# The last two weight blocks of an output projection, multiplied chunk by chunk

## The reference, cut to what matters

```python
def rmsnorm(x, g):
    xf = x.astype(jnp.float32)
    y = xf * lax.rsqrt(jnp.mean(xf * xf, axis=-1, keepdims=True) + RMS_EPS)
    return (y * g.astype(jnp.float32)).astype(x.dtype)

f = swiglu(rmsnorm(h, ffn1_g_pre[l]), ffn1_w_gu[l], ffn1_w_down[l])
h = h + MACARON_W * rmsnorm(f, ffn1_g_post[l])
m = hybrid_mixer(rmsnorm(h, mix_g_pre[l]), mix_w_in[l], ...)
h = h + rmsnorm(m, mix_g_post[l])
```

## Time and profile before

| | |
|---|---|
| median of 3 runs | 1300.17 us (1297.37 to 1300.36) |
| the profiled execution, its time | 1300.92 us |
| its span | 1299.2 us |
| PE busy | 1236.9 us (95%) |
| POOL busy | 493.9 us (38%) |
| ACT busy | 448.5 us (35%) |
| DVE busy | 414.1 us (32%) |
| mean granted clock of TensorE | 0.973 |

### The profile page before, as it was taken

The page is one execution under the profiler, slowest core; times in us unless marked ns, Lnnn a source line. Parts: engine busy times, 40 slices in busy tenths (PEclk is TensorE's granted clock), DMA queues, the critical chain, the costliest instruction groups (busy, mean ns, idle before and its releaser), DMA issues.

```text
span 1299.2 us, 15515 instructions
## 1 busy us (share of the span) xinstructions
PE 1236.9 (95%) x5659; PEld 1001.6 (77%) x5659; DVE 414.1 (32%) x708; ACT 448.5 (35%) x688; POOL 493.9 (38%) x238
## 2 busy tenths in 40 slices
PE   7999999999998989999989899889899999999997
PEld 5788888888886667777767877667788888888886
DVE  4432222210017353544351424521722323230004
ACT  3433333331134344453333444423532323231113
POOL 4344444444442331222133673214244444444442
PEclk9999999999998988999889899999999999999999
DMA  5233333222231221111102342102133333322211
GB/s 183 65 98 97 97 97 97 97 97 97 97 97 49 65 70 45 49 49 49 66 28 89 114 151 81 58 32 86 61 98 98 97 97 97 97 96 91 93 60 65
DMA packets 83319, 108.76 MB, mean 84 GB/s; under 512 B 8686, under 2 KB 53836, under 8 KB 83276
## 3 DMA queue, kind: packets, MB, share of 16 engines
q1 hardware_dynamic: 83120, 108.14, 25.6%
q10 hardware_dynamic: 156, 0.04, 0.0%
HBM read 106.06 MB, written 2.10 MB: 83 GB/s over the span
## 4 chain that ended last, share of the span: by engine, by line
PE 42%; issue 38%; POOL 14%; DVE 4%; ACT 2%; POOLq 0%; DVEq 0%; ACTq 0%
PE bank L1409 13%; POOL w_lo L563 13%; PE bank L1411 13%; PE bank L1410 13%; PE bank L1427 1%; PE bank L1417 1%; DVE acc L983 1%; DVE acc L980 0%; PE bank L1434 0%; DVE h L1040 0%; DVE f_fin L1394 0%; DVE qm_lo L1176 0%; ACT xh L640 0%; DVE tmp L1168 0%; ACT w_hi L627 0%
## 5 line engine op out<-in xcount | busy, mean ns | idle before, releaser
L563 POOL TENSOR_TENSOR w_lo<-raw,w_hi 128x1024 fp32r<-128x1024 f32 x176 | 428.2, 2433 | 750.1 <-ACT w_hi L627 750.1
L1409 PE MATMUL bank<-xh,w_hi 128*128 128x512 f32 x992 | 394.3, 397 | 16.6 <-DVE xl L969 14.5
L1411 PE MATMUL bank<-xh,w_lo 128*128 128x512 f32 x992 | 389.7, 393 | 0.0
L1410 PE MATMUL bank<-xl,w_hi 128*128 128x512 f32 x992 | 389.2, 392 | 0.0
L627 ACT ACTIVATE w_hi<-raw 128x1024 fp32r<-128x1024 f32 x176 | 186.3, 1058 | 512.6 <-PE bank L1411 508.1
L1409 PEld LDWEIGHTS bank<-xh,w_hi 128*128 128x128 f32 x992 | 188.2, 190 | 63.2 <-issue 17.0
L1411 PEld LDWEIGHTS bank<-xh,w_lo 128*128 128x128 f32 x992 | 187.9, 189 | 39.9
L1410 PEld LDWEIGHTS bank<-xl,w_hi 128*128 128x128 f32 x992 | 188.3, 190 | 37.6
L1409 PE MATMUL bank<-mid_hi,w_hi 128*128 (+1 forms) x352 | 138.9, 394 | 0.0
L1411 PE MATMUL bank<-mid_hi,w_lo 128*128 (+1 forms) x352 | 138.0, 392 | 0.0
L1410 PE MATMUL bank<-mid_lo,w_hi 128*128 (+1 forms) x352 | 136.6, 388 | 0.0
(11 more groups left out here) (234 smaller groups left out, 1337.1 us busy)
## 6 DMA issues: line engine op xcount, KB each, us to landing
raw<-in_ffn_w_gu SPq DMA_DIRECT2D x176, 256.0 KB, 2.9
raw<-in_ffn_w_down SPq DMA_DIRECT2D x88, 256.0 KB, 2.8
raw<-in_mix_w_in SPq DMA_DIRECT2D x48, 256.0 KB, 2.8
raw<-in_mem_w_kv SPq DMA_DIRECT2D x32, 256.0 KB, 3.3
raw<-in_mix_w_out SPq DMA_DIRECT2D x16, 256.0 KB, 3.0
raw<-in_mem_w_q SPq DMA_DIRECT2D x16, 256.0 KB, 3.2
raw<-in_mem_w_o SPq DMA_DIRECT2D x16, 256.0 KB, 2.8
x_tok<-in_x SPq DMA_DIRECT2D x4, 512.0 KB, 5.0
```

The costliest lines, as they stand in the source:

```text
L563: gp.tensor_tensor(w_lo[:, n % SPLIT, :], raw[:, n % RAW, :], w_hi[:, n % SPLIT, :].bitcast(F32), ALU.subtract).then_inc(lo_ready, 1)
L1409: pe.matmul(dst, w[0], x[0], start=start, stop=False, skip_group_check=loose)
L1410: pe.matmul(dst, w[0], x[1], start=False, stop=False, skip_group_check=loose)
L1411: return pe.matmul(dst, w[1], x[0], start=False, stop=stop, skip_group_check=loose)
```

## The change

A new function of PE, `closing_out`, takes the last two weight blocks of each output projection together: for each bank first the three products of block n-1, then the three of block n. Each bank so ends with its six products. In bank 7, between the two triples, stand the four products that sum `acc`, with the flag that clears bank 0; the squares of banks 6 and 7 are summed after the last product, as before. In the SwiGLU the loop has one turn fewer, and three blocks are written out behind it. On ACT one rounding is no longer issued before the squares. The diff, without its unchanged parts:

```diff
...
                 round_to(OUT_END[s])
                 act.preload_act_table(ACT.Sqrt)
-                round_to(OUT_END[s] + 1)
                 act.wait_ge(hacc_ready, H_ADDS * (s + 1))
                 for m in range(DC):
                     wait_out(act, s, m)
...
                 for _ in range(products):
                     pe.matmul(dst[:, :], ones[:, :], ones[:, 0:1].to_broadcast([P, SEQ]), start=True, stop=True)
-            def token_sums(dst, parts):
+            def token_sums(dst, parts, first=True, last=True):
...
                     for semaphore, count in waits:
                         pe.wait_ge(semaphore, count)
                     for t in range(TC):
-                        last = pe.matmul(dst[:, t:t + 1], square[:, t * P:(t + 1) * P], ones[:, 0:1],
-                                         start=n == t == 0, stop=n == len(parts) - 1, skip_group_check=True)
-                return last
+                        done = pe.matmul(dst[:, t:t + 1], square[:, t * P:(t + 1) * P], ones[:, 0:1],
+                                         start=first and n == t == 0, stop=last and n == len(parts) - 1,
+                                         skip_group_check=True)
+                return done
             def spread(dst, src):
...
                     pe.wait_ge(saved_a, 1)
                     turn_h(2)
                 token_sums(out_bank(s, 0), [
-                    (fsq(DC - 2), [(f0_saved, s + 1), (fsq_ready, DC * s + DC - 1)]),
-                    (acc, [(facc_ready, F_ADDS * (s + 1))]),
-                    (fsq(DC - 1), [(fsq_ready, DC * (s + 1))])]).then_inc(fstat, 1)
+                    (fsq(DC - 2), [(fsq_ready, DC * s + DC - 1)]),
+                    (fsq(DC - 1), [(fsq_ready, DC * (s + 1))])], False).then_inc(fstat, 1)
                 if s == SUBLAYERS - 1:
                     pe.wait_ge(saved_a, 2)
                     turn_h(3)
...
                 if DC - 1 in ms:
                     last.then_inc(w_used, 1)
+            def closing_out(s, n, x):
+                w = [weights(n - 1), weights(n)]
+                for m in range(DC):
+                    cols = slice(m * P, (m + 1) * P)
+                    for j in range(2):
+                        last = three(out_bank(s, m)[:, :], (w[j][0][:, cols], w[j][1][:, cols]), x[j],
+                                     False, j == 1, True)
+                        if m == DC - 1:
+                            last.then_inc(w_used, 1)
+                            if j == 0:
+                                token_sums(out_bank(s, 0), [
+                                    (acc, [(f0_saved, s + 1), (facc_ready, F_ADDS * (s + 1))])], True, False)
+                    if m < DC - 1:
+                        last.then_inc(out_done, 1)
             def swiglu(s, up, down):
                 first = 2 * FG * (s // 3)
                 first_block(s, up, 0)
...
                 pe.wait_ge(up_scaled, first + 2 * FG - 1)
                 pe.wait_ge(midl_done, first + 1)
                 out_block(s, down, hidden(0), True, False, free={4: (up_scaled, first + 2 * FG + 1)})
-                with pe.Fori(0, (FC - 2) // 4) as i:
+                with pe.Fori(0, (FC - 6) // 4) as i:
                     for k in range(4):
                         pe.wait_ge(midl_done, at_turn(i, 4, first + 2 + k))
                         out_block(s, down + 1 + k, hidden(at_turn(i, 4, 1 + k)), False, False, i, 4)
+                for k in range(FC - 5, FC - 2):
+                    pe.wait_ge(midl_done, first + 1 + k)
+                    out_block(s, down + k, hidden(k), False, False)
                 pe.wait_ge(midl_done, first + FC)
-                out_block(s, down + FC - 1, hidden(FC - 1), False, True)
+                closing_out(s, down + FC - 1, (hidden(FC - 2), hidden(FC - 1)))
                 out_stat(s)
             def fill(turn):
...
                 for k in range(2):
                     free = {0: (gfactor, GLA_H), 2: (mem_l, DC)} if k == 0 else {}
                     group_block(B_OUT + 2 + k, k, 0, (fox_hi, fox_lo), free=free, last_chunk=DC)
-                for c in range(4, DC):
+                for c in range(4, DC - 2):
                     pe.wait_ge(y_l, Y_FOX + c - 3)
-                    out_block(1, B_OUT + c, (xh[:, c, :], xl[:, c, :]), False, c == DC - 1)
+                    out_block(1, B_OUT + c, (xh[:, c, :], xl[:, c, :]), False, False)
+                pe.wait_ge(y_l, Y_GLA)
+                closing_out(1, B_KV - 1, [(xh[:, c, :], xl[:, c, :]) for c in (DC - 2, DC - 1)])
                 out_stat(1)
             def memory():
...
                 attention(MEM_B)
                 free = {3: (pt_l, N_UNITS), 5: (y_l, Y_GLA + 7), 6: (y_l, Y_GLA + DC)}
-                for c in range(DC):
+                for c in range(DC - 2):
                     pe.wait_ge(y_l, Y_GLA + c + 1)
-                    out_block(2, B_MO + c, (xh[:, c, :], xl[:, c, :]), c == 0, c == DC - 1,
+                    out_block(2, B_MO + c, (xh[:, c, :], xl[:, c, :]), c == 0, False,
                               free={} if c else free, ms=range(DC) if c else range(3, DC))
+                pe.wait_ge(y_l, Y_GLA + DC)
+                closing_out(2, B_UP2 - 1, [(xh[:, c, :], xl[:, c, :]) for c in (DC - 2, DC - 1)])
                 out_stat(2)
```

## The result

The changed kernel takes 1317.47 us (median of 4 runs, 1314.87 to 1322.54), the kernel before, in runs beside it, 1298.77 us. The ratio is 1.0157 (95% interval 1.0130 to 1.0184): slower by 18.7 us, the difference of the medians. The prediction had 1322.0 us, 21.8 us over before, with a range from 1316 to 1328, and slower at 0.97.

A forecast was written before the change was run, and what follows sets the result against it. The prediction took TensorE (PE), busy for 95% of the span, as the bound. Added waits 15.3, clock 6.0 and ends 0.5 made 21.8 us, giving a median of 1322.0 us, with a range from 1316 to 1328.

The forecast's parts named there:

- The wait that is added: Before block n-1 of each projection, PE waits for block n's weights: 3.80 or 3.86 us each, 15.3 us together.
- The clock: Behind each of the four added pauses PE's clock falls: 1.5 us each, 6.0 us, one pause bounded by 0 and 2.0.
- The ends: After each projection's last product, POOL's residues delay the update of h: three ends of 0.17 us, 0.5 us together.
- E + 7.43: At the first projection's end, POOL's two residues end 7.43 us after E, the end of the last weight product before.
- The sum: Whole kernel: 15.3 + 6.0 + 0.5 = 21.8 us slower, median 1322.0 us; the forecast's chance was 0.70.
- Rival 2: The clock costs more, 2.0 us or more at each pause and some low stretches at ends: 1328 us, chance 0.09.
- Rival 1: At the four pauses the clock doesn't fall, or falls while PE stands: 1316 us, chance 0.13.
- Rivals 3 and 5: Respectively: PE waits for `acc` in the closing stretch, 1325 us, 0.04; the wait comes only before block n, 1319 us, 0.02.
- Rival 4: Faster: three ends without the wait for DVE, the sums and one rounding give 8.4 us, 1291.8 us; chance 0.02.

The follow-up runs named there:

- e1: The kernel before, with only PE's wait for the last block's weights added ahead of block n-1 at each projection; 1322.05 us, ratio 1.0191.
- e2: The changed kernel, with a third slot for each projection's last block so its rounding waits for block n-3, not n-2; 1299.68 us, ratio 1.0012.
- e3: The changed kernel, with the sums of `acc` put back behind the last product; 1319.64 us, ratio 1.0153.
- e10: The changed kernel, with DVE's eight operations on GLA's output waiting for POOL to complete the mixer's fourth output block; ratio 1.0154.
- e4: The kernel before, with ACT's part of the change alone: the next stage's first block is rounded behind the squares; 1295.02 us, ratio 0.9968.
- e7: The kernel before with ACT's part of the change alone, the same kernel as e4 measured once more; 1294.32 us, ratio 0.9965.
- e8: The kernel before, with ACT's first rounding behind the squares, its second behind the next pre-norm's second chunk, and DVE waiting for POOL in the mixer; ratio 0.9961.

## Why the prediction was right, and where it was off

- **The wait that is added** (15.3 us): the four steps from block n-2 to block n-1 grew by 15.4 us. Right, and e1 shows that it is the cause.
- **The clock** (6.0 us, 1.5 for each pause): too small. In the changed kernel the 48 products took 12.2 us more, of which the sums are 4.2 by e2, so the clock took 8.0; in e1 it took 6.3, in e3 9.6, in e10 8.3. The mean is 8.0, 2.0 us for a pause, with 1.3 to 2.9 in the sixteen. The step that was off is the one that took 1.5 because "part of the low stretch can pass during the pause itself". In the changed kernel it did so at the fourth pause, which cost 1.3 us. At the second and third it did too, but there the clock stayed low for 6.8 us in all, and the loss was 2.5 us each; the first cost 1.7. None of the sixteen pauses escaped. By the rule of the Trainium skill (TensorE: Matmul & The Clock Gate, "HAM oscillation — how this bites in real kernels") none does, and the sixteen agree; its 6.8 us in the sum were nearer than 6.0. The upper bound of 2.0 us from the pause of 5.14 us was too low as a bound.
- **The ends** (+0.5 us): with the sums' 4.2 us counted, the ends changed by -4.2 + 4.2 = 0. The sum is right within what low clock moves from profile to profile; the single ends, each with what e2's 48 products took more, are -0.2, -0.4, +0.5 and +0.1. `acc` didn't wait, but the reason given, the slower banks, isn't shown (e4). Two roundings filled the time before the root (it came 2.4 us after the last product, 2.6 in the prediction), and the update of h ended 0.56 us behind POOL (0.54 in the earlier trace rows). One comparison in the prediction was wrong: it set POOL's end, E + 7.43, against the start of the update before, E + 7.26. By its own rows the update ends 0.54 us behind POOL, at E + 7.97, against 395.76 + 0.75 = E + 8.01 before, so that the loss of 0.17 us was none. In the changed kernel the first update ends 6.86 us behind the last product, and with the sums' 0.99 us that is E + 7.85. The Trainium skill (SBUF — State Buffer, "Who interferes with whom") says that a DVE instruction with two SBUF inputs contends with a GpSimd one that reads SBUF; the update of 1.46 us in place of 0.75 agrees. The prediction's "for a whole instruction" is too short for the mixer, where a residue of 2.4 us took 6.76, beside the rest of DVE's eight instructions.
- **The sum** (21.8 us): the four projections of the two profiles differ by 23.4 us. Measured were 18.7 by the medians and 20.4 by the ratio (16.9 to 23.9), and the three variants with the same pauses, e1, e3 and e10, gave 23.8, 21.4 and 22.1 by the medians. The forecast time is 4.5 us above the measured median, 1.4 us of it from the baseline. The rest of the program differs between profiles by as much (4.6 us in this pair); the forecast had no term for that, and that the median still lies within the range, 1.5 us above its lower end, is partly luck.
- **The rivals.** Rival 2, the clock costing more, had the price of the pauses right (8 us), but its time of 1328 is further off than the forecast. Rival 1's time, 1316, is nearer to the median than the forecast is, so the time alone doesn't rule it out; the rows with the clock at 0.50 behind each pause do. Rivals 3 and 5 are out: nothing waits before `acc`, and the pauses of 3.65 to 3.71 us stand before block n-1. Rival 4, the faster kernel, failed as stated: its 0.92 us of sums can't be removed by moving them. But a part of it can be had without the new order: the rounding ahead of the squares cost DVE 1.2 us through POOL, which I had in the trace as the 0.83 us before `acc` and read as DVE being slow. e4 gets it without any pause.

## What to carry to other kernels

A step that takes two buffers of a ring of two has no ring left: ask when the second one is filled, and what used to run meanwhile. Moving work of PE from behind the last product to between products doesn't shorten PE's path, it only moves the work along it. What can be gained is the time that PE waits for another engine, and the cheapest such gain here was one instruction in ACT's order, since it moved POOL away from DVE. Take a change apart before dropping it: one half of this one was worth 0.3 to 0.4% (e4, e7), the other cost 1.9% (e1).

## What the runs showed of the hardware that I had not expected

Pauses of the same length cost different amounts. Behind the first, of 3.65 us, the granted clock was 0.50 for 3.41 us; at the second, of 3.71 us, it went to 0.50 in the pause and stayed there for 6.83 us. At all sixteen pauses of 3.6 to 3.7 us ahead of block n-1 the clock fell. At the program's start a pause of 3.2 us could escape: in e1 the clock stayed at 1.00 from 19.29, where such a pause ended, to 31.1; in e8 it was at 0.50 from 20.2 to 23.6, behind one that ended at 18.97. And an engine can be shut out by a row of the other's instructions, not only by one: POOL's residue of 2.4 us took 6.76 us behind DVE's eight operations, and 2.60 us when it came in after the first, with 4.71 us instead of 2.49 for DVE's first four.
